# v rows of three gather passes moved to TensorE in pairs of buffers, and one set of query weights loaded once

## What is computed

```python
q = (xt @ w_q).reshape(T, PEER_HEADS, 2, PEER_HALF)
s = jnp.einsum('thcd,hcnd->thcn', q, sub_keys)
...                      # two top-16 lists, sums of pairs, top 16 of them
expert_idx = ...         # (T, 8, 16): 128 picks of a token out of 16384 experts
gates = jax.nn.softmax(top_s, axis=-1)
...
ub = jnp.take(u, eb, axis=0)
act = jax.nn.gelu(jnp.einsum('thkd,td->thk', ub, xb), approximate=False)
vb = jnp.take(v, eb, axis=0)
return jnp.einsum('thk,thkd->td', gb * act, vb)
```

## Time and profile before

| | us |
|---|---|
| median of 3 runs | 2250.74 |
| lowest and highest | 2244.51, 2264.61 |
| span of the profiled execution, first to last instruction | 2259.6 |
| gathers under way, from pass 0's first to the end of pass 7 | 208 to 1937 |
| tail after the last gather | 320 |

### The profile page before, as it was taken

One profiled execution on the slowest core, in us unless ns is written; L12 is line 12 of the kernel. 1 busy time (PEld: TensorE's weight loads), 2 busy tenths in 40 slices (PEclk: granted clock), 3 DMA queues, 4 the chain that ended last, 5 costly groups with the idle time before them and its releaser, 6 DMA issues. The chain is left out here.

```text
span 2259.6 us, 17114 instructions
## 1 busy us (share of the span) xinstructions
PE 1527.2 (68%) x5282; PEld 879.4 (39%) x5282; DVE 1450.5 (64%) x3168; ACT 323.1 (14%) x778; POOL 985.0 (44%) x1058
## 2 busy tenths in 40 slices
PE   8987600467656539776573897666576656899998
PEld 7446600222225225422341552235252232376453
DVE  1236898779587875678688468786978676444101
ACT  1220100011112111111120111111321000123111
POOL 0102466667665555566455456653446444000000
PEclk9989855688867669987766899778767877899999
DMA  7436999999999999999999999999989999973672
GB/s 260 85 117 245 394 408 409 337 360 370 371 379 403 404 406 358 361 365 367 407 399 405 365 342 368 375 401 386 391 293 403 399 398 399 366 243 130 242 260 93
DMA packets 268005, 760.62 MB, mean 337 GB/s; under 512 B 21295, under 2 KB 46590, under 8 KB 267275
## 3 DMA queue, kind: packets, MB, share of 16 engines
q0 software_dynamic: 147456, 536.94, 61.8%
q1 hardware_dynamic: 120458, 222.60, 27.8%
HBM read 756.84 MB, written 2.62 MB: 336 GB/s over the span
## 5 line engine op out<-in xcount | busy, mean ns | idle before, releaser
L946 POOL DMA_INDIRECT ROWS<-in_peer_u,IDX x512 | 483.3, 944 | 455.5 <-DVE ROWS L991 266.9
L946 POOL DMA_INDIRECT ROWS<-in_peer_v,IDX x512 | 487.8, 953 | 357.2 <-PE bank L292 121.4
L991 DVE SCALAR_TENSOR_TENSOR ROWS<-ROWS,XP 128x1024 f32<-128x1024 f32 x512 | 602.3, 1215 | 23.7 <-issue 12.3
L995 DVE SCALAR_TENSOR_TENSOR XP<-ROWS,GATE,XP 128x1024 f32<-128x1024 f32 x316 | 405.8, 1284 | 155.9 <-DMA ROWS<-in_peer_v,IDX 133.7
L292 PE MATMUL bank<-ROWS,DG 128*128 128x512 f32 x774 | 380.0, 649 | 94.2 <-DMA ROWS<-in_peer_v,IDX 78.5
L292 PE MATMUL bank<-ring,XT 128*128 128x512 f32 (+6 forms) x912 | 392.7, 589 | 62.3 <-DMA ring<-in_ffn_w_up 32.0
L292 PEld LDWEIGHTS bank<-ring,XT 128*128 128x128 f32 x912 | 185.6, 214 | 249.9 <-issue 179.4
L292 PEld LDWEIGHTS bank<-ROWS,DG 128*128 128x128 f32 x774 | 157.5, 209 | 309.8 <-issue 201.8
L292 PE MATMUL bank<-XT,ring 128*128 128x128 f32 (+2 forms) x1504 | 209.4, 301 | 57.1 <-issue 27.4
L292 PEld LDWEIGHTS bank<-XT,ring 128*128 128x128 f32 (+1 forms) x1504 | 198.3, 204 | 71.8 <-issue 35.7
L307 PE MATMUL bank<-CN,X 128*128 128x128 f32 x128 | 27.1, 384 | 184.9 <-issue 90.7
(11 more groups left out here) (408 smaller groups left out, 1461.6 us busy)
## 6 DMA issues: line engine op xcount, KB each, us to landing
ring<-in_peer_w_q SPq DMA_DIRECT2D x16, 2048.0 KB
ring<-in_ple_w_gate SPq DMA_DIRECT2D x9, 2048.0 KB
ring<-in_ffn_w_gate SPq DMA_DIRECT2D x8, 2048.0 KB
ring<-in_ffn_w_up SPq DMA_DIRECT2D x7, 2048.0 KB
ring<-in_a_w_in SPq DMA_DIRECT2D x6, 2048.0 KB
ring<-in_w_in SPq DMA_DIRECT2D x6, 2048.0 KB
ring<-in_ffn_w_down SPq DMA_DIRECT2D x6, 2048.0 KB
ROWS<-in_peer_u,IDX POOLq DMA_INDIRECT x512
```

What stands on the lines that cost most here:

```text
L946: G.indirect_dma_start(ROWBUF[slot(n, c)][:, :], None, tables[table], bass.IndirectOffsetOnAxis(IDX[:, tt, c:c + 1], axis=0)).then_inc(row ...
L991: V.scalar_tensor_tensor(row, row, 1.0, XP[:, :], ALU.mult, ALU.mult, accum_out=ACTV[:, tt, c:c + 1]).then_inc(row_used, 1)
L995: V.scalar_tensor_tensor(XP[:, :], row, gate, XP[:, :], ALU.mult, ALU.add).then_inc(row_used, 1)
```

## The change

- In passes 1, 3 and 5 TensorE takes all 128 picks, VectorE and ScalarE none; the diagonals `DG` go.
- The rows of these passes are gathered in another layout. Four buffers (a group, `GROUP = 4`) hold four picks of 128 tokens in all, as before, but buffer q holds all four picks for the 32 tokens of quarter q (`QUAD = 32`): partition 32 k + t is pick k of token 32 q + t. So the index list is turned: `pe_to_quads` does it on TensorE with 16 small products, `dve_turn_picks` copies the result to `IDXV`, and GpSimd waits for `picks_turned`. The gates are turned in the same way in two halves (`gv0`, `gv1`), and `dve_spread` multiplies them with a 0/1 pattern into stationary operands of 128 x 32, kept in `SPREAD` (and `Y` for the third quarter), 4096 columns in all.
- `pe_share` now takes a group in two pairs of buffers, (0, 1) and (2, 3). Each buffer's product has 32 stationary columns and writes PSUM partitions 32 q to 32 q + 31 of `accA`, then of `accB`. One increment of `pe_used` frees both buffers of a pair. The first two groups are done inside `weigh`; in `peer_route` four groups stand between two blocks of queries.
- `dve_sums` adds x and the two banks directly; the next u pass's first two rows are taken before it.
- `peer_q01_` goes from the stream. Three blocks of `peer_q0_` stay in the ring until tile 1 has read them, the fourth (`KEPT`) lies in row buffers 8 to 11. In pass 0 the gathers 8 to 11 wait until tile 1's product with it has been read (`kept_read`).
- Constants used only in the first stage lie in `ROWS` (`CN_EARLY`) to make room.

```diff
-DIAGS = 4
+GROUP = 4
+QUAD = P // GROUP
+KEPT, KEPT_SLOT = 3, RING + MORE - 1
...
+            for e in range(4):
+                enter(f"peer_q{tag}_{e}", cols(a["peer_w_q"][l], 512 * e, 512 * e + 512), KEPT_SLOT if (l, e) == (0, KEPT) else None)
...
-        enter_cols("peer_q01_", a["peer_w_q"][0], [0, 512, 1024, 1536, 2048])
...
-            return n in SHARED and c % (2 * RUN) >= RUN
+            return n in BY_PE
...
+                if n == 0 and c * D // SLOT == KEPT_SLOT - RING:
+                    G.wait_ge(S("kept_read"), 1)
+                picks = IDXV if n in BY_PE else IDX
...
+        def pe_to_quads(src, name):
...
+            for k in range(GROUP):
+                for q in range(GROUP):
+                    last = mul(b[QUAD * k:QUAD * k + QUAD, q:GROUP * m:GROUP], ident[:, QUAD * q:QUAD * q + QUAD],
+                               src[:, k:GROUP * m:GROUP], True, True)
...
+        def dve_spread(n, half):
...
+            for x in (2 * half, 2 * half + 1):
+                gates = result(name)[:, QUAD * (x % 2):QUAD * (x % 2) + QUAD]
+                V.tensor_tensor(spread(tt, x), con("spread").unsqueeze(1).broadcast_to([P, QUAD, QUAD]),
+                                gates.unsqueeze(2).broadcast_to([P, QUAD, QUAD]), ALU.mult).then_inc(spread_ready, 1)
...
+                for pair in ((0, 1), (2, 3)):
+                    for q in pair:
+                        PE.wait_ge(*arrived(n, GROUP * g + q))
+                    for q in pair:
+                        to, row = slice(QUAD * q, QUAD * q + QUAD), ROWBUF[slot(n, GROUP * g + q)]
+                        last = mul(accs[0][to, :], weights[:, j + q, :], row[:, 0:512], first, end)
...
+                            last = mul(accs[1][to, :], weights[:, j + q, :], row[:, 512:1024], first, end)
+                    last.then_inc(pe_used, 1)
...
         def dve_sums(n):
...
+            V.wait_ge(*nth("x_copied", 2))
+            gather_begin(n + 1)
+            gather_some(2)
             V.wait_ge(pe_used, tensor_used(n))
...
-                V.tensor_tensor(y, y, result(name)[:, :], ALU.add).then_inc(bank_free(name), 1)
+                V.scalar_tensor_tensor(Y[:, tt, s], X[:, tt, s], ALPHA, result(name)[:, :], ALU.mult, ALU.add).then_inc(bank_free(name), 1)
...
+                        pe_to_quads(GATE[:, tt, half], f"gv{i}")
+                    pe_share_begin(n + 1)
+                    pe_share(n + 1, 0, 2)
...
-                        pe_share(beside, 6 * e, 6 * e + 6)
+                    if l == 1 and e > 0:
+                        pe_share(beside, 4 * e - 2, 4 * e + 2)
...
+                    for e in (KEPT, *range(KEPT)):
+                        queries(slot_of(f"peer_q{tag}_{e}"), tt, e)
+                        weight_read(f"peer_q{tag}_{e}", f"q{e}{tt}")
```

More of the change, by code:

```diff
@@ L489, in end_phase @@
             base.update(count)
-            jobs.clear()
+            for name in [k for k in jobs if not (held and k in ("accA", "accB"))]:
+                del jobs[name]
         PE = nc.tensor
@@ L564, in _ @@
                         sp.dma_start(bias[:, :, T:T + P], bass.AP(scratch.tensor, 2 * P - 1, [[width - 1, P], [P * width, NH], [1, P]])).then_inc(S("bias_in"), 16)
-                    before = [m for m in range(n) if slot_no[m] == slot_no[n]]
-                    if before:
+                    before = [m for m in range(n) if slot_no[m] == slot_no[n] and m not in beside_ring]
+                    if n in beside_ring:
+                        sp.wait_ge(S("phase_end"), 3)
+                    elif before:
                         sp.wait_ge(*released[before[-1]])
@@ new lines, in pe_share @@
+        def pe_share(n, g0=0, g1=PICKS // GROUP):
+            accs, tt = (result("accA"), result("accB")), passes[n][1]
+            for g in range(g0, g1):
+                first, end = g == 0, g == PICKS // GROUP - 1
+                x, j = divmod(GROUP * g, QUAD)
+                PE.wait_ge(spread_ready, 4 * (n // 2) + x + 1)
+                weights = spread(tt, x)
+                for pair in ((0, 1), (2, 3)):
[4 more added lines that the diff above has]
+                        last = mul(accs[0][to, :], weights[:, j + q, :], row[:, 0:512], first, end)
+                    if end and 3 in pair:
+                        last.then_inc(bank_ready("accA"), 1)
+                    for q in pair:
+                        to, row = slice(QUAD * q, QUAD * q + QUAD), ROWBUF[slot(n, GROUP * g + q)]
+                        if end and q == GROUP - 1:
+                            held.clear()
+                            mul(accs[1][to, 0:256], weights[:, j + q, :], row[:, 512:768], False, True).then_inc(bank_ready("accB"), 1)
+                            last = mul(accs[1][to, 256:512], weights[:, j + q, :], row[:, 768:1024], False, True)
+                        else:
+                            last = mul(accs[1][to, :], weights[:, j + q, :], row[:, 512:1024], first, end)
+                    last.then_inc(pe_used, 1)
```

165 lines of the change are left out of this document (94 added, 71 removed).

## The result

The changed kernel took 2279.14 us (median of 4 runs), the kernel before beside it 2252.65 us: a ratio of 1.010, 95% interval 1.0053 to 1.0146. The ratio leaves out one slow run of the changed kernel (2449.39 us, at a granted clock of 0.67 where the others had 0.81); the other three have a median of 2276.94 us. Forecast were 2208 us and a gain of 43 us; it lost about 24 (12.1 between the two profiled spans, 2271.7 against 2259.6). On another chip the same kernel was later 0.4% faster than the kernel before, so it also has to be asked why the sign depends on the chip.

What follows compares the result with a forecast made beforehand. DMA bounds the u passes; TensorE freeing row buffers late bounds the v passes. Terms -16 - 20 - 11 + 3 - 2 + 3 = -43 us from the median 2250.7 gave 2208 us, range 2165 to 2258.

Steps and rivals of the forecast that it cites:

- What sets a v pass is how late TensorE frees a row buffer.: Passes 1, 3, 5: GpSimd waits 21.3, 48.7, 51.4 us for TensorE; windows 30, 49, 49 us over the 159 us floor.
- -16 of pass 1: Pass 1: GpSimd loses 14 us early, then nothing waits; 173 us against 188.8.
- Rows on TensorE: Passes 1, 3, 5: two neighbouring products run side by side, a pair costs 1.76 us, 0.88 per buffer.
- The rival of tiles that don't overlap: TensorE's rows in v passes: 1.76 us a buffer, pass 1 +55, passes 3 and 5 +80 each, 2455 us; chance 0.12.
- the one of visible loads: TensorE's weight loads show, 1.15 us a buffer, passes 3 and 5 gain nothing: 2230 us; no-change chance 0.15 in all.
- A step is now 16 buffers, 16 x 0.88 = 14.1 us, plus the block beside it, on average 12.1: 26.2.: TensorE's cycle in passes 3 and 5: 26.2 us where GpSimd needs 19.8; four cycles lose 25 us.
- -10 for each pass: Passes 3 and 5: 198 us against 208, -20 together.
- End of a v pass, -11: Sums end some 2 us after the last landing, next u rows don't wait: 4 + 4 + 3 us gained.
- VectorE's part: Rows removed are worth nothing by themselves; added spread products cost nothing in passes 2 and 4, some 3 in pass 0: +3.
- Query weights and pass 0, -2: Pass 0: loading query weights once saves a 5.1 us wait, holding gathers 8 to 11 costs +3; bounds -21 and +10.
- small things: More instructions on TensorE and other buffers in the ring: +3 us.
- Time given back: Passes' gains handed on to VectorE-bound stages, besides weight loads that show: 2240 us; no-change chance 0.15 in all.

Runs made afterwards that it cites:

- e4: Changed kernel, each row product on TensorE taking 64 of its 512 columns, on chip A: 2246.54 us in one run, pass 1 186.4 us.
- e16: Changed kernel, each row product on TensorE taking 64 of its 512 columns, on chip D: 2261.11 us in one run, pass 1 187.8 us.
- e3: Changed kernel, 16 buffers of a cycle in two steps of 8, ahead of and behind each block of queries, on chip A: ratio 0.9982 to the kernel before.
- e15: Changed kernel, 16 buffers of a cycle in two steps of 8, on chip D: ratio 0.9999 to the kernel before.
- e12: Changed kernel, steps of 8, VectorE's later waits for sums and turned picks, three query-weight blocks kept in the ring, one loaded again, chip C: ratio 0.9914.
- e11: Changed kernel, steps of 8 buffers and VectorE's later waits for sums and turned picks, spread products in their old place, chip C: ratio 0.9979.
- e1: Changed kernel with the first layer's query weights loaded a second time for tile 1, no block in row buffers, on chip A: ratio 1.010.
- e13: Changed kernel with the first layer's query weights loaded a second time for tile 1, no block in row buffers, on chip D: ratio 1.0099.
- e14: Changed kernel, three query-weight blocks kept in the ring for tile 1, the fourth loaded again, none in row buffers, on chip D: ratio 1.0088.
- e5: Changed kernel, GpSimd passing two more long-satisfied waits ahead of each gather of passes 1, 3 and 5, on chip B: ratio 0.9984.
- e7: Kernel before the change, GpSimd passing two more long-satisfied waits ahead of each gather of passes 1, 3 and 5, on chip B: ratio 1.0004.
- e2: Changed kernel with steps of 12 buffers instead of 16 between blocks of queries in passes 3 and 5, on chip A: ratio 1.0057.

## Why the prediction was wrong

**"What sets a v pass is how late TensorE frees a row buffer."** Wrong for pass 1. I took GpSimd's 21.3 us of waits as TensorE's work and its windows' 30 us over the floor as the room. e4 and e16 take that work away and pass 1 doesn't move. The row named the engine rightly and the reason wrongly: TensorE's matmuls were done, and GpSimd went on up to 9 us after their end. I could have seen it in the profile before: the gather at 497.06 (above) waited 4.1 us for a buffer freed 6.7 us earlier. I didn't hold one wait against the end of the matmul it waited for. The -16 of pass 1 measured -1.7. Where increments are prompt there was no such room either: the kernel before takes 169.6 us there, less than the 173 forecast for the changed one, and the change took 2.1 off it.

**Rows on TensorE.** The mechanism was right and the size too cautious: a pair whose buffers stand ready costs 0.90 us and not 1.76, since its tiles also run beside those of the next pair; alone it takes 1.91, close to the 1.76 of the two-tile case. The rival of tiles that don't overlap is out. So is the one of visible loads: the page's group has these loads at 114 ns each, and with 0.11 us for each of the 48 matmuls none of them can stand in between. The Trainium skill's rule on loads of the same row group ("TensorE: Matmul & The Clock Gate", Part 3) does not hold in this trace; the measurement decides. But this term had no room to act, as above.

**"A step is now 16 buffers, 16 x 0.88 = 14.1 us, plus the block beside it, on average 12.1: 26.2."** The cycles measured 28.6, 30.4 and 30.7 us. The step took 16.9 and 15.9 us although its arithmetic is 7.2, because of the wait inside it for the ring of 12 to fill again; I summed TensorE's costs and never asked where the 13th buffer comes from. The block's 12.1 was a stretched one: on chip C it is 7.4 us for the queries and 1.1 for the scores, and in the changed kernel's first profile the queries alone take 10.9, 13.7 and 15.9 behind the steps. The three long stops at gathers 36, 52 and 68 of pass 3 cost 9.0, 10.8 and 11.2 us of GpSimd where I had 6.4 a cycle; on chip C, with the same steps and the same wait inside them, they cost 7.0, 5.5 and 3.2. So where the blocks aren't stretched, 6.4 was about right, though by another way; what the sum lacked is mostly their stretching. -10 for each pass measured -1.5 and +0.7, and -6.3 and -7.2 on chip C. Another order of the steps gives back 5 us or more of it on chips A and D (e3, e15). (Rows 4 give a cycle of 24.0 us before the change, (918.99 - 847.05) / 3, and not 23; the sum doesn't rest on it.)

**End of a v pass, -11, and "passes 2 and 4 are held by the DMA engines".** The hand-over came: VectorE's first u row starts 5.5 us after the pass's first gather and not 13.9 (pass 2). But a u pass ends with VectorE's row 117, whose buffer the next pass's first gather takes, and from row 1 to row 117 it needed 210.2 us where it had needed 194.8: the sums moved inside (1.3 us and a wait of 3.0), the copy of the picks (0.3 and 2.6), two spread products (2.4), and longer waits in its old places. Busy time over the window, "40 us to spare", was no reserve, since those 40 us are waits in a chain of its own. Passes 2 and 4 measured +7.0 and +6.1 where I had -4 each, and +3 for all of VectorE's part; pass 6 measured -7.5 where I had -3. On chip C, with prompt increments and none of the new waits, passes 2 and 4 still lose 4, about what the instructions take that now stand between their rows.

**Query weights and pass 0, -2.** Measured +6.7 in the first pair of profiles, where VectorE has the three waits shown above, and -2.4 on chip C, where it has none of the two new ones. GpSimd's wait for `kept_read` was 14.7 us and not 3; it cost 6.5 us on chip C (e12 against e11), and nothing that shows on chips A and D (e1, e13, e14). The +3 for small things has no row behind it, and no run shows it.

**The rivals.** "Time given back" named the right direction at 2230 to 2240 and stopped at zero. I didn't ask of each of the change's new hand-overs between engines what it costs if it takes 8 us instead of 0.5, as the profile before could have told me: 180 of its increments have no record within 1 us, and GpSimd's stop at 497.06 shows that this was waited out.

What stays open: why increments are late and TensorE's matmuls are spaced out on chips A and D. That both occur together, in every kernel run there, and not on B and C, is shown; no experiment reached the cause. The two that were to reach it (e5, e7) ran on a chip without it. There is a rival that no run tests: records are missing on these chips too, and whatever loses them may hold up the engines as well. And that the late increments make pass 1 some 20 us longer is argued, from 23 us of stops where they occur and 167.5 us where they don't; e4 shows only that TensorE's work does not.

## What to carry to other kernels

A wait that is put down to an engine is to be held against the end of the very instruction it waited for; if that had ended long ago, giving the engine less work will change nothing. A step that takes more buffers than the ring has waits inside for the refill, which a sum of the engine's costs leaves out; but here cutting the step to the ring gained nothing (e2), and splitting it gained on one sort of chip only. And a change that trades one engine's time for more hand-overs between engines stands or falls with what a hand-over costs on the chip at hand: here 1.010 on a chip of one sort and 0.996 on a chip of the other.

## What was not expected of the hardware

On two of the four chips an engine that waited for TensorE went on up to 9 us after its matmuls' end while gathers ran (8.2 and 8.7 us in the two places shown above); on the other two no profile has more than one of TensorE's increments without a record within 1 us. The kernel before is 3% slower on the former (2260 to 2264 us against 2193 to 2195), at nearly the same granted clock (0.80 to 0.81 against 0.81 to 0.82). The traces of the former also lack half of the gathers' landing records. And consecutive pairs of 32-column products overlap, four at a time: 48 matmuls of 512 moving columns in 5.38 us, 0.11 us each, where 24 with 128 stationary columns took 10.54.
